# Hybrid mLSTM/attention/GLA/conv step with a mixture of experts: two picked experts, a sorted last place, two spare weight rooms

## The reference, cut to what matters

```
def _hier_moe(h, p):                       # h: 384 tokens x 1024, float32
    gl = h @ w_group_router                # 4 groups: the best one
    el = h @ w_expert_router               # 16 experts: the best two inside that group
    ...                                    # softmax weights of the two
    for each expert (16): y += (silu(h @ e1) * (h @ e3) * weight) @ e2
                                           # e1, e3: 1024 x 512; e2: 512 x 1024
```

## Time and profile before

| | |
|---|---|
| median of 3 runs | 1884.13 us (1882.58 to 1886.51) |
| the profiled execution | 1894.46 us, span 1892.7 us |
| TensorE busy | 1782.1 us, 94% |
| VectorE, ScalarE, GpSimd busy | 813.7, 442.7, 122.4 us |
| mean granted TensorE clock | 0.972 |
| bytes moved | 422.42 MB, mean 223 GB/s |

### The profile page before, as it was taken

How to read it: one execution, slowest core, us unless ns; L and a number is a source line. 1 busy time by engine, 2 the same in 40 slices (tenths; PEclk the granted TensorE clock), 3 DMA queues, 4 the chain that set the end, 5 groups by cost and what they waited for, 6 DMA issues and landing times.

```text
span 1892.7 us, 25310 instructions
## 1 busy us (share of the span) xinstructions
PE 1782.1 (94%) x10202; PEld 1095.7 (58%) x10202; DVE 813.7 (43%) x1850; ACT 442.7 (23%) x956; POOL 122.4 (6%) x160
## 2 busy tenths in 40 slices
PE   6999999999999989997789999999999998999887
PEld 3445656688777773332245565667888877333223
DVE  1295473565544451111133966536655455111113
ACT  3312344333100121010043134334321112111002
POOL 0001201000000030000020020010000003000002
PEclk9999999999999989998989999999999998999988
DMA  9662293413556658999952221323123335899994
GB/s 403 224 261 91 95 361 106 156 68 112 198 221 270 245 200 353 425 427 426 424 209 101 110 94 58 131 93 120 69 90 112 133 151 201 326 424 425 428 427 156
DMA packets 51926, 422.42 MB, mean 223 GB/s; under 512 B 6448, under 2 KB 7872, under 8 KB 28768
## 3 DMA queue, kind: packets, MB, share of 16 engines
q1 hardware_dynamic: 33696, 369.35, 48.9%
q0 software_dynamic: 9632, 33.07, 5.1%
q10 hardware_dynamic: 8480, 18.35, 2.6%
HBM read 386.38 MB, written 32.28 MB: 221 GB/s over the span
## 4 chain that ended last, share of the span: by engine, by line
PE 81%; DMA 14%; another core or an unknown queue 1%; issue 1%; DVE 1%; ACT 1%; SPq 0%; POOL 0%; ACTq 0%; DVEq 0%
PE psum L871 19%; PE psum L1148 19%; PE psum L1137 9%; PE psum L1319 8%; PE psum L874 7%; DMA pc<-we_in 6%; DMA ring<-we_in 6%; PE psum L1340 2%; PE psum L791 2%; PE psum L1324 2%; DMA ring<-wch_in 2%; PE psum L849 1%; PE psum L1223 1%; PE psum L1335 1%
## 5 line engine op out<-in xcount | busy, mean ns | idle before, releaser
L871 PE MATMUL psum<-hT,ring 128*128 128x384 f32 x1088 | 363.9, 489 | 0.1
L871 PEld LDWEIGHTS psum<-hT,ring 128*128 128x128 f32 x1088 | 202.9, 190 | 141.2 <-issue 12.4
L1137 PE MATMUL psum<-pc,ring 128*128 128x384 f32 x512 | 175.6, 486 | 0.0
L1319 PE MATMUL psum<-ring,scr 128*64 128x512 f32 x512 | 126.9, 653 | 30.9 <-DMA ring<-we_in 27.1
L2625 DVE TENSOR_TENSOR ytok<-pc,psum 128x256 f32<-128x256 f32 (+1 forms) x32 | 15.1, 471 | 323.1 <-ACT pc L1815 323.1
L1148 PE MATMUL psum<-hT,ring 128*128 128x192 f32 x768 | 143.0, 329 | 1.8 <-ACT vals L1514 1.8
L1148 PEld LDWEIGHTS psum<-hT,ring 128*128 128x128 f32 x768 | 126.1, 190 | 18.6 <-issue 9.6
L1319 PE MATMUL psum<-pc,scr 128*64 128x512 f32 x512 | 118.0, 615 | 18.7 <-DMA pc<-we_in 18.7
L2015 DVE SCALAR_TENSOR_TENSOR pc<-pc,par 128x384 f32<-128x384 f32 x240 | 127.2, 605 | 0.0
L874 PE MATMUL psum<-ring,hT 128*128 128x512 f32 x288 | 125.2, 593 | 0.0
L1137 PEld LDWEIGHTS psum<-pc,ring 128*128 128x128 f32 x512 | 94.4, 190 | 51.9
(11 more groups left out here) (421 smaller groups left out, 2383.8 us busy)
## 6 DMA issues: line engine op xcount, KB each, us to landing
ring<-we_in SPq DMA_DIRECT2D x48, 2048.0 KB, 17.8
pc<-we_in SPq DMA_DIRECT2D x48, 2048.0 KB, 20.0
ring<-wch_in SPq DMA_DIRECT2D x18, 2048.0 KB, 8.3
ring<-wgate_in SPq DMA_DIRECT2D x16, 2048.0 KB, 8.4
ring<-wmod_in SPq DMA_DIRECT2D x18, 1024.0 KB, 6.7
pc<-wmod_in SPq DMA_DIRECT2D x24, 768.0 KB, 7.7
ring<-wbr_in SPq DMA_DIRECT2D x16, 1024.0 KB, 4.8
ring<-wtok_in SPq DMA_DIRECT2D x6, 2048.0 KB, 8.9
```

Source lines behind the costliest of these rows:

```text
L871: mm = pe.matmul(F[:, 0:T], wv[:, k, n * P:(n + 1) * P], hT[:, k, :], start=k == 0, stop=k == KD - 1)
L1137: mm = pe.matmul(bank(7)[:, 0:T], wv[:, c, (n % 4) * P:(n % 4 + 1) * P], pc[:, MERGE_SLOT[i], c, :], start=c == 0, stop=c == 3)
L1319: mm = pe.matmul(bank(2)[BIG * h:BIG * h + BIG, :], x_h[:, k, 0:BIG], w[h][:, k, :], start=k == 0, stop=k == KD - 1, skip_group_check=True)
```

## The change

Four things are changed, all in the experts' part.

1. Two more rooms for input weights (`spare_rooms`): one of parameters and `t_last`, one of new memory (`late_room`) and `ytok`. The third of every three places (2, 5, 8, 11, 14) reads its two input blocks there, in four DMAs of 12 KB and 4 KB for each partition. Input blocks are now read for place e+3 when `hidden(e)` is over, and those of place 2 as soon as the order is known. The memory comes from GpSimd's descriptor room, which is set to 4096 bytes per partition; for that the zeroing of the row tensors is cut from 2 DMAs to 12.
2. Experts 0 and 1 are both picked on the chip. The 0/1 matrix is now stationary (64 or 32 columns) and the tokens move (512 or 256 columns). The rows then come unturned, are copied to SBUF, and are turned like those of other places.
3. The last place is sorted too (`FREE` has 14 places), it is the smallest expert, and it is computed for 64 rows, as two halves side by side. `last_one` marks which expert it is; its row numbers and weights are found by sums over the 16 experts.
4. `hidden(15)` comes ahead of `project(14)`, on TensorE and VectorE. `store_rows(14)` comes behind the copy of `turn_hidden(15)` on ScalarE.

```diff
+def expert_slot(e, j):
+    return 3 * (e % 2) + 2 if j == 2 else 3 * (e % 3) + j          # spare(e): e % 3 == 2
-FREE = range(2, NE - 1)
+FREE = range(2, NE)
+        last_one = sb("last_expert", [P, 1, NE])
+        late_room = sb("late_room", [P, 3072])
+        spare_rooms = ((par[:, work:work + 3072], last_and_zeros[:, :]),
+                       (late_room[:, :], ytok[:, 0:2, :].rearrange("p t n -> p (t n)")))
+            def fill_spare(l, e):
+                for j, rooms in enumerate(spare_rooms):
+                    src, of = block_of(l, ("exp", e, j)), 0
+                    for room in rooms:
+                        width = room.shape[-1]
+                        sp.dma_start(room, src[:, of:of + width]).then_inc(rest_in.sem, 16)
+                        of += width
                 sp.wait_ge(slot_ready.sem, slot_ready.at(l, 2))
-                for e in range(NE - 1):
-                    ...
-                    if e < NE - 2:
-                        sp.wait_ge(xab_done.sem, xab_done.at(l, e + 1))
-                        fill(l, ("exp", e + 2, 0))
-                        if e < NE - 3:
-                            fill(l, ("exp", e + 2, 1))
+                for e in range(-1, NE - 1):
+                    if e + 3 < NE:
+                        ...
+                        if e >= 0:
+                            sp.wait_ge(xab_done.sem, xab_done.at(l, e + 1))
+                        elif l == 0:
+                            sp.wait_ge(rows_zeroed.sem, ZEROED)
+                        fill_inputs(l, e + 3)
                     if e >= 1:
                         sp.wait_ge(xy_done.sem, xy_done.at(l, parts_to(e)))
                         fill(l, ("exp", e + 1, 2))
-                    if e == NE - 3:
-                        fill(l, ("exp", NE - 1, 1))
@@ TensorE: the picks
-                for k in range(KD):
-                    for t in range(NT):
-                        mm = pe.matmul(x_turned[:, k, :], htok[:, t, k * P:(k + 1) * P], first_pick[:, t * P:t * P + CAP], ...)
+                for e in range(2):
+                    pe.wait_ge(pick_ready.sem, pick_ready.at(l, e + 1))
+                    for b, size, lo, width in ((0, BIG, 0, 512), (1, SUB, BIG, 256)):
+                        for t in range(NT):
+                            one = first_picks[e][:, t * P + lo:t * P + lo + size]
+                            for c in range(P // size):
+                                mm = pe.matmul(bank(4 * e + b)[size * c:size * c + size, 0:width], one,
+                                               htok[:, t, c * width:(c + 1) * width], ...)
+                    mm.then_inc(xt_done.sem, 1)
+                turn_rows(0)
@@ TensorE: the end of the loop
+                hidden(NE - 1)
                 for n in range(2 if wide(NE - 2) else 1):
                     project(NE - 2, n)
-                hidden(NE - 1)
                 ...                                       # the branch on spilled, turn_hidden(15)
+                project(NE - 1, 0)
                 for t in range(2):
-                    project(NE - 1, t)
                     pe.wait_ge(mix_ready.sem, mix_ready.at(l, t + 1))
@@ ScalarE
+                ac.wait_ge(xt_done.sem, xt_done.at(l, 1))
+                for b, picked_rows in enumerate(x_rows[0]):
+                    ac.activation(picked_rows, bank(b)[:, 0:512 // (b + 1)], ACT.Copy).then_inc(ht_copied.sem, 1)
                 copy_rows(0)
                 ac.wait_ge(scattered.sem, scattered.at(l, scattered.per_layer))
-                load_rows(1)
                 load_rows(2)
                 for e in range(NE):
-                    if e == NE - 1:
-                        store_rows(e - 1)
                     ...                                   # SiLU, copy_rows(e + 1), load_rows(e + 3), branch, copy
-                    if 1 <= e < NE - 1:
+                    if e >= 1:
                         store_rows(e - 1)
@@ VectorE
-                for t in range(NT):
-                    o = ve.tensor_scalar(first_pick[:, tok(t)], cc("iota"), rk[:, t, 0:1], None, ALU.is_equal)
+                for e in range(2):                        # 2 x 3 matrices of 128 x 96
+                    ...
-                step(ve.memset(rmul[:, :, NE - 1:NE], 1.0))
+                step(ve.tensor_scalar(last_one[:, 0, FREE.start:FREE.stop], rank, float(RANK_AT[-1]), None, ALU.is_equal))
+                step(ve.tensor_tensor(rmul[:, :, :], rmul[:, :, :], of_last, ALU.max))
+                for of, to in ((rk, v1), (rw, v2)):       # row number and weight of the last place
+                    step(ve.tensor_tensor(sel[:, :, :], of[:, :, :], of_last, ALU.mult))
+                    step(ve.tensor_reduce(to, sel[:, :, :], AX.X, ALU.add))
+                ...                                       # the same pair for the rows to read back, twice
+                ve.wait_ge(xt_done.sem, xt_done.at(l, 2))
+                for b, picked_rows in enumerate(x_rows[1]):
+                    o = ve.tensor_copy(picked_rows, bank(4 + b)[:, 0:512 // (b + 1)])
-                keep_out(NE - 2)
                 open_hidden(NE - 1)
+                keep_out(NE - 2)
@@ GpSimd and the build
+                    for i in range(0, NE * CAP // P * 4, ZERO_PIECE):   # ZERO_PIECE = 8: 6 DMAs for each tensor
-    nc = bacc.Bacc("TRN2", target_bir_lowering=False, num_devices=1)
+    nc = bacc.Bacc("TRN2", target_bir_lowering=False, num_devices=1, dynamic_dma_scratch_size=4096)
```

More of the change, by code:

```diff
@@ L126, in weight_uses @@
         plan += [(("out", 0), 0), (("out", 1), 1)]
-        plan += [(("exp", e, j), 3 * (e % 2) + j) for e in range(NE) for j in range(3)]
+        plan += [(("exp", e, j), expert_slot(e, j)) for e in range(NE) for j in range(3) if j == 2 or not spare(e)]
         uses += [((l, key), slot) for key, slot in plan]
@@ L193, in rows_loaded @@
 def rows_loaded(i):
-    return sum(32 if wide(j) else 16 for j in range(1, i + 1) if j % 2 == i % 2)
+    return sum(32 if wide(j) else 16 for j in range(2, i + 1) if j % 2 == i % 2)
 CTX, LAT = slice(0, SEQ), slice(SEQ, T)
@@ L1315, in hidden @@
                         pe.wait_ge(xg_ready.sem, xg_ready.at(l, e))
-                    w = [have(l, ("exp", e, j)) for j in range(2)]
+                    if spare(e):
+                        pe.wait_ge(rest_in.sem, 16 + 64 * (l * len(range(2, NE, 3)) + e // 3 + 1))
+                        parts = [[r.rearrange("p (k n) -> p k n", n=512) for r in rooms] for rooms in spare_rooms]
+                        w = [[r[:, k, :] for r in rooms for k in range(r.shape[1])] for rooms in parts]
+                    else:
+                        w = [[have(l, ("exp", e, j))[:, k, :] for k in range(KD)] for j in range(2)]
                     for k in range(KD):
                         for h in range(2):
-                            mm = pe.matmul(bank(2)[BIG * h:BIG * h + BIG, :], x_h[:, k, 0:BIG], w[h][:, k, :],
+                            mm = pe.matmul(bank(2)[BIG * h:BIG * h + BIG, :], x_h[:, k, 0:BIG], w[h][k],
                                            start=k == 0, stop=k == KD - 1, skip_group_check=True)
@@ L2768, in _ @@
                 if l == 0:
-                    gp.wait_ge(rows_zeroed.sem, 32)
+                    gp.wait_ge(rows_zeroed.sem, ZEROED)
                 for n in range(1, KD - 1):
```

121 lines of the change are left out of this document (70 added, 51 removed).

## The result

The changed kernel takes 1946.41 us, median of 4 runs (1941.84 to 1953.02); the kernel before took 1883.36 beside it (4 runs, 1882.15 to 1886.51). The ratio is 1.0335, 95% interval 1.03 to 1.0369. The forecast was 1886.0, at most 1894; the change is slower by 63 us. The other 9 us stand in no trace: the profiled execution of the kernel before was 10 us longer than its median, that of the changed kernel 2 us.

What follows compares the result with a forecast made beforehand. From place 2 on, experts were taken to wait for weights at 426 GB/s. Layer 0: -1.3 + 2.2 + 0.8 = +1.7; layer 1: -2.9 + 3.0 = +0.1; together +1.8 us, median 1884.1 to 1886, range 1875 to 1894.

Steps and rivals of the forecast that it cites:

- The zeroing ... has nothing else to do then; taken as 0.: GpSimd may wait between the 12 zeroing DMAs: taken as 0, up to some 6 us of GpSimd alone.
- I take 717.0: Head of layer 0: scatter beside weights ends between 710.2 and 717.6, taken 717.0; SiLU(0) +3.6 us, in layer 1 +2.7.
- rival C: Head: weights are served first, the scatter ends at 720, SiLU(0) 3 us later still; +6, 1892; chance 0.08.
- The picks' part: Head: picks of two experts, partly at half clock, then turning; `hidden(0)` ends +2.9 us in layer 0, +0.3 in layer 1.
- equal-packets reading: Head: equal packets would give the scatter half the rate, an end near 714, and SiLU(0) 0.8 us earlier.
- At half clock each chunk takes twice its 0.76 us. I take 2.2 us a layer.: Very end of each layer: chunks start at half clock after TensorE's idle time; 2.2 us a layer, between 0 and 3.4.
- the head start: Place 2's blocks read earlier: 9.9 us to win in each layer, of which 6.3 and 7.2 us remain after the head.
- The tail's sum: Tail, after block 13 lands: `project(13)`, transposes, `hidden(15)` and `project(14)` take 14.8 us before place 14's output can be copied.
- the moved product's price: Tail: 14.8 us of TensorE work before place 14's copy, against 3.65 for `project(14)` alone; price 11.2 us.
- First gather to chunks: Tail: six gathers in a row 13 us, plus ScalarE 1.15 and VectorE 1.28; 15.5 us, before 19.5 and 19.4.
- The branch gap of 1.6 us: Tail: SiLU(15) came 1.6 us after its product; the branch may now hold `project(14)`'s copy; 0 or 1.6, taken 0.8.
- my rivals: Chances: head start arrives, whole or half, 0.31; moved product decides 0.21; scatter starves 0.08; change fails to do as said 0.04.

Runs made afterwards that it cites:

- e1: The changed kernel with its zeroing moved ahead of the first mask of layer 0; 1927.33 us, ratio 1.0183 to the kernel before.
- e5: The kernel before with only the smaller descriptor room (4096) and the zeroing cut into 12 pieces; ratio 1.0055.
- e2: The changed kernel with the chunks' last product reading its operands on 96 partitions again, not 64; 1915.75 us, ratio 1.0104.
- e3: The changed kernel with 35 unread products per layer filling TensorE's idle time before the chunks, still on 64 partitions; 1935.76 us, ratio 1.0209.
- e4: The changed kernel with the reads of place 2's weights held until the scatter has landed; 1932.52 us, ratio 1.021.
- e6: The changed kernel with ScalarE's wait for the scatter and the row loads of places 2 and 3 moved to the end of place 0; 1930.3 us, ratio 1.0199.
- e7: The changed kernel with `hidden(15)` behind `project(14)` again, stores and copies in their old order; 1930.59 us, ratio 1.0182.
- f1: The kernel before with the chunks' last product reading 64 partitions in place of 96; ratio 1.0063.
- f2: The kernel before with only `hidden(15)` moved ahead of `project(14)`, stores and copies in the changed order; 1913.72 us, ratio 1.0123.
- e9: The changed kernel with zeroing moved earlier, ScalarE's scatter wait behind place 0, old end order and chunks on 96 partitions; 1888.05 us, ratio 1.0025.

## Why the prediction was wrong

Three steps failed, all in the same direction. Of the others most held, some of them by luck.

1. **"The zeroing ... has nothing else to do then; taken as 0."** The step that failed by kind. GpSimd has nothing else to do, but its queue has: the state store stands behind the last three pieces and ScalarE waits for it. +12.2 us; e1 takes it away, and e5 makes 5.5 us of it alone in its trace, 10.5 on the medians. My bound of 6 us looked at GpSimd waiting, not at what is queued behind.

2. **"I take 717.0" for the scatter's end.** The mechanism was named (ScalarE held by the scatter, `hidden(1)` behind SiLU(0)), the size was not. I added the bytes of both and divided by 426 GB/s, 17.2 us, and took this as the far bound; the scatter took 24.2 and 28.1 (23 to 24 in the other runs), beyond my rival C's 720 too. The rate was wrong, since beside the row writes the engines moved some 300 GB/s for 8 us. And nothing then bounded it: in layer 0 the next fills were issued at 730.26, with the scatter still open. So SiLU(0) came 9.0 and 12.2 us late, not 3.6 and 2.7. The picks' part of it came out: `hidden(0)` ended +2.7 and +0.4 us against the first pick, foretold +2.9 and +0.3. That was partly luck. In e1, e2, e3, e4, e6 and e7, with the same picks, it ended 25.9 to 28.8 us behind the first pick, in the changed kernel 23.6 and 22.2, before 21.0 and 21.8.
   The Trainium skill (DMA: Bandwidth & Descriptors, Queues, rings and completion order) says the engines go round by packets. By the prediction's equal-packets reading of it the scatter would have taken some 16 us (an end near 714), and no run here agrees with that.

3. **"At half clock each chunk takes twice its 0.76 us. I take 2.2 us a layer."** Measured 12.6, as two mistakes. I did not see that fewer partitions make the product slower: 1.10 us in place of 0.76 at full clock (f1, e3), 1.98 in place of 1.50 at half (e2). And my 2.2 us stands for a half clock of some 4 us, in line with the 5 us of the earlier trace rows; its upper bound of 3.4 has no row behind it. On 64 partitions the half clock lasted through all 16 us and into the norm.

Against this the head start came, if not whole. The two blocks were issued before 714, and from SiLU(0) to the block of place 13 it took 215.0 and 215.8 us, foretold 212.7 and 211.7. The tail's sum was near: from the start of `project(13)` to the end of `project(14)` it took 14.5 us in layer 0, foretold 14.8, so the moved product's price is 10.8 us where I had 11.2. First gather to chunks was foretold 15.5 us and is 16.2 and 15.6; `project(13)` to the first gather was foretold 21.2 and is 19.9 and 22.7, in layer 1 with a `project(13)` of 6.41 us after an idle of 4.70. The branch gap of 1.6 us went away and wasn't moved. With points 1 to 3 at their measured sizes my sum gives +12.2, +5.4 + 9.5 and 2 x 10.4 more, 1.8 + 47.9 = 49.7 of the 54.0. The last 4 are mostly the place-13 blocks, 2.3 and 4.0 us later behind SiLU(0) than in my walk, less some 2 us of smaller terms.

The sum had no row for the order by itself. f2 shows that in the kernel before it costs 11 us a layer, and e7 that it still costs 2 to 5 us in the changed one, so the fourth part of the change was a loss in this kernel.

None of my rivals had the zeroing or the 64 partitions in it, so the range could not hold the time.

## What to carry to other kernels

When a DMA queue's descriptor room is cut or a transfer is split, look for what stands behind it on that queue and who waits for it; the issuing engine's idle time is no cover. A wait for a slow transfer belongs behind what doesn't need it: moving ScalarE's wait was worth as much as making the scatter twice as fast. But it must not go so far back that the rows behind it come late, as in e9. And a matmul need not be cheaper for reading fewer partitions; price the form that will run, at the clock it will find, from a row of that form.

## What the runs showed of the hardware that I had not expected

- A product with 64 rows of both operands (128 columns held, 384 moved, f32) took 0.42 us from start to start, with 96 rows 0.32, at the same granted clock of 1.0.
- On 64 rows, busy without a pause, TensorE was granted 0.50 (1.2 GHz) for 16 us; on 96 rows it went from 0.50 to 1.0 (2.4 GHz) 4 to 6 us into the same sequence (e2, e9). Where the clock was 1.0 as the sequence began, it stayed so on 64 rows as well (e3, f1: 9 us). Why 64 rows differ here is not shown.
- 3.15 MB written row by row took 10.8 to 12.7 us alone and 23 to 28 us beside 4.19 MB of weights, more than the 17.2 us that both together would take at 426 GB/s. In the first 8 us the engines were full and moved some 300 GB/s (changed kernel, 712 to 720 us).
- With a descriptor room of 4096, GpSimd issued three zeroing pieces and then waited 10.4 to 16.1 us before the next three (changed kernel, e5), and 13.9 to 23.4 us in e1's place for them.
